# Hybrid attention/DeltaNet block on one core: block read-back moved to SyncE, gate differences and spread moved, other slots for convolutions and FFN input

## What is computed

```
proj = xn @ w_in                       # 2048 x 7184
dn_qkv = silu(causal_dwconv(dn_qkv, dn_conv_w))          # width 4
g = cumsum over a chunk of 64;  decay = exp(g_i - g_j) where i >= j
L = tril(k_beta @ k^T * decay);  T = inv(eye + L)
u = T @ v_beta;  w = T @ (k_beta * exp(g))               # then a scan over chunks
mix = concat(rmsnorm(attention), rmsnorm(o_dn) * silu(z)) @ w_out
ffn: (gelu(gate) * val) @ w_down, with gate, val = split(causal_dwconv(h @ w_up) + b)
```

## Time and profile before

| | |
|---|---|
| median of 3 runs | 1251.06 us (1250.89 to 1254.26) |
| profiled execution, its time | 1252.81 us |
| its span | 1251.1 us |
| TensorE busy | 1226.1 us, 98% |
| VectorE, ScalarE, GpSimd busy | 877.2, 738.8, 214.9 us |
| granted TensorE clock, mean | 0.997 |
| DMA over the span | 183 GB/s |

### The profile page before, as it was taken

The page is one execution under the profiler, slowest core; times in us unless marked ns, Lnnn a source line. Parts: engine busy times, 40 slices in busy tenths (PEclk is TensorE's granted clock), DMA queues, the critical chain, the costliest instruction groups (busy, mean ns, idle before and its releaser), DMA issues.

```text
span 1251.1 us, 20175 instructions
## 1 busy us (share of the span) xinstructions
PE 1226.1 (98%) x6651; PEld 1051.1 (84%) x6651; DVE 877.2 (70%) x1633; ACT 738.8 (59%) x1454; POOL 214.9 (17%) x254
## 2 busy tenths in 40 slices
PE   8899999999999999999999999999999999999997
PEld 6787897889888888788888888888888888888886
DVE  5878866754444754788878888887887885555554
ACT  7767558544867555666566656656656554444442
POOL 1120511141103000022222322222232220000000
PEclk9999999999999999999999999999999999999999
DMA  9647332842443655255455455555555565555551
GB/s 375 254 154 244 138 127 92 251 140 103 148 154 135 218 188 200 103 202 199 173 199 198 168 201 182 189 189 184 195 183 193 194 236 186 186 200 203 185 185 67
DMA packets 35909, 228.91 MB, mean 183 GB/s; under 512 B 6528, under 2 KB 6928, under 8 KB 9232
## 3 DMA queue, kind: packets, MB, share of 16 engines
q1 hardware_dynamic: 34016, 223.50, 50.2%
q10 hardware_dynamic: 1840, 4.71, 1.2%
HBM read 225.96 MB, written 2.24 MB: 182 GB/s over the span
## 4 chain that ended last, share of the span: by engine, by line
PE 85%; DVE 5%; ACT 3%; DMA 3%; issue 2%; POOL 1%; SPq 1%; DVEq 0%; ACTq 0%; POOLq 0%
PE bank L1334 32%; PE bank L1338 16%; PE bank L1362 10%; PE bank L1360 10%; PE bank L1361 10%; DVE w_lo L896 2%; DMA arena<-in_x_tok 2%; DMA arena<-base_rows 1%; DVE arena L917 1%; PE bank L1479 1%; ACT w_hi L464 1%; PE bank L1472 1%; PE bank L1455 1%; PE bank L1639 1%; PE bank L1637 1%
## 5 line engine op out<-in xcount | busy, mean ns | idle before, releaser
L896 DVE TENSOR_TENSOR w_lo<-raw,w_hi 128x512 fp32r<-128x512 f32 x816 | 574.8, 726 | 263.6 <-ACT w_hi L464 259.3
L464 ACT ACTIVATE w_hi<-raw 128x512 fp32r<-128x512 f32 x816 | 502.2, 630 | 356.3 <-PE bank L1334 176.8
L1334 PE MATMUL bank<-xhl,w_hi 128*128 128x512 f32 x2044 | 659.7, 399 | 5.4 <-DVE arena L901 2.7
L1338 PEld LDWEIGHTS bank<-xhl,w_lo 128*128 128x128 f32 x2044 | 384.8, 188 | 88.0
L1338 PE MATMUL bank<-xhl,w_lo 128*128 128x256 f32 x2044 | 402.4, 278 | 0.0
L1334 PEld LDWEIGHTS bank<-xhl,w_hi 128*128 128x128 f32 x2044 | 317.1, 189 | 7.3 <-DVE w_lo L896 3.3
L1361 PE MATMUL bank<-w_lo,ffn_act 128*128 128x512 f32 x336 | 130.7, 389 | 0.0
L1360 PE MATMUL bank<-w_hi,ffn_act 128*128 128x512 f32 x336 | 130.7, 389 | 0.0
L1362 PE MATMUL bank<-w_hi,ffn_act 128*128 128x512 f32 x336 | 130.7, 389 | 0.0
L434 POOL TENSOR_TENSOR arena<-arena,token_scale 128x256 f32<-128x256 f32 x88 | 78.1, 902 | 302.9 <-DVE arena L901 192.5
L1258 DVE SCALAR_TENSOR_TENSOR arena<-arena,fcw 128x256 f32<-128x256 f32 x176 | 85.3, 485 | 23.9 <-DVE arena L1255 1.5
(11 more groups left out here) (239 smaller groups left out, 1005.6 us busy)
## 6 DMA issues: line engine op xcount, KB each, us to landing
raw<-in_wts SPq DMA_DIRECT2D x203, 1024.0 KB, 4.8
xfeat<-in_x SPq DMA_DIRECT2D x4, 512.0 KB, 8.6
arena<-in_x_tok SPq DMA_DIRECT2D x1, 2048.0 KB, 19.8
xfeat<-in_x_tok SPq DMA_DIRECT2D x1, 2048.0 KB, 9.2
arena<-base_rows ACTq DMA_DIRECT2D x4, 512.0 KB
out_y<-xfeat SPq DMA_DIRECT2D x8, 256.0 KB, 2.0
arena<-gate_rows SPq DMA_DIRECT2D x1, 1024.0 KB, 4.2
arena<-in_post_gains ACTq DMA_DIRECT2D x1, 1024.0 KB, 6.1
```

What stands on the lines that cost most here:

```text
L464: nc.scalar.activation(w_hi[:, i % RING, :], raw[:, slot, quarter * PIECE:(quarter + 1) * PIECE], ACT.Copy).then_inc(hi_ready, 1)
L896: V.tensor_tensor(w_lo[:, i % RING, :], raw[:, slot, quarter * PIECE:(quarter + 1) * PIECE], w_hi[:, i % RING, :].bitcast(f32), ALU.subtra ...
L1334: return M(ps[j][:, :], w_hi[:, r % RING, kk * P:(kk + 1) * P], xhl[:, k, :, :].rearrange("p a t -> p (a t)"), start=(k == 0), stop=(k == ...
L1338: return M(ps[j][:, 0:T], w_lo[:, r % RING, kk * P:(kk + 1) * P], xhl[:, CHUNK_K * q + kk, 0, :], start=False, stop=False, skip_group_chec ...
```

## The change

SyncE reads the base blocks back itself, behind its stores and ahead of the next weight chunk. The gate differences of batch 1 are made at places 92 to 95 (before: 100 to 103), and their exponential stands between `qs` and `z1`. VectorE spreads the base columns, at places `_l + 32` and `_l + 33`. Row sums, gates and the turned logits stand one place later. Taps of the convolutions of groups 3 to 5 stand at 1, 4, 7, 10 of their group, the SiLU at 12. In the output norm, one residual tile stands ahead of the last evacuation, both in the mixer and in the FFN. `WARM` is 7.

```diff
-WARM = 8
+WARM = 7
-SILU_AT = [10, 9, 10, 15, 15, 15]
-CONV_AT = [(3, 5, 7, 9)] + [(1, 3, 5, 7)] * 2 + [(1, 5, 9, 13)] * 3
+SILU_AT = [10, 9, 10, 12, 12, 12]
+CONV_AT = [(3, 5, 7, 9)] + [(1, 3, 5, 7)] * 2 + [(1, 4, 7, 10)] * 3
-PLACE = {"ba": 10, "stat": 14, "ba_turn": 16, "scale": 15, "gate": 21, "gcum": 24, "grow": 28}
+PLACE = {"ba": 10, "stat": 15, "ba_turn": 17, "scale": 16, "gate": 21, "gcum": 25, "grow": 28}
...
-        PLACE["spread", _b, _g] = _l + 35
-        PLACE["turn", _b, _g] = _l + 37 + _g
+        PLACE["spread", _b, _g] = _l + 32 + _g
+        PLACE["turn", _b, _g] = _l + 36 + _g
...
+for _i in range(BH):
+    PLACE["dm", _i] = 34 + _i
+    PLACE["dm", BH + _i] = 92 + _i
+PLACE["dexp", 0], PLACE["dexp", 1] = 39, 98
@@ sync, behind the eight stores of a batch
+                sp.wait_ge(s("scratch_in"), 16 * NBLK * (b + 1))
+                for jh in range(2):
+                    rows_ = slice(jh * BASE // 2, (jh + 1) * BASE // 2)
+                    sp.dma_start(block_l[:, rows_].rearrange("p j u i -> p (j u i)"),
+                                 scratch[b].rearrange("(n j) (o x) -> n o j x", j=BASE, o=1)[:, :, rows_, :].rearrange(
+                                     "n o j x -> n o (j x)").to_broadcast([NBLK, BASE, BASE * UNITS * BASE // 2])
+                                 ).then_inc(s(f"block_in{jh}"), 16)
@@ scalar
-                follow(PLACE["load", b])
-                act_e.wait_ge(s("scratch_in"), 16 * NBLK * (b + 1))
...
                 scaled_columns(lambda i: otok[b][:, 2 * i + 1, :], ps[7], EG, 1, "qs_sb")
+                if b == 0:
+                    decay(1)
                 follow(PLACE["z1", b])
@@ vector, behind the last row step (the same product stood on gpsimd)
+                dve.wait_ge(s("base_row"), BASE * (b + 1))
+                for g in range(2):
+                    follow(PLACE["spread", b, g])
+                    V.tensor_tensor(
...
+                if b == 0:
+                    gate_difference(1)
                 follow(PLACE["ks", b])
@@ vector, mixer to FFN
-                out_tile(NB - 1, j)
...
             dve.wait_ge(s("row_root"), 3)
-            dve.wait_ge(s("m_evac"), NJ * NB)
             hidden(1, 0)
+            out_tile(NB - 1, 1)
             hidden(1, 1)
@@ vector, end
-                down_tile(NB - 1, j)
                 dve.wait_ge(s("row_root"), j + 5)
-                dve.wait_ge(s("f_evac"), NJ * (NB - 1) + j + 1)
+                dve.wait_ge(s("f_evac"), NJ * (NB - 1) + j)
                 for c in range(NB):
+                    if c == 1:
+                        down_tile(NB - 1, j)
+                    if c == NB - 1:
+                        dve.wait_ge(s("f_evac"), NJ * (NB - 1) + j + 1)
                     residual(down, 2, j, c * 512, (c + 1) * 512, "y_ready")
```

More of the change, by code:

```diff
@@ L395, in _ @@
                                    pattern=[[0, UNITS], [1, P]], channel_multiplier=-1).then_inc(s("dmask"), 1)
[L396 to L403, removed]
                 for i in range(2 * LEVELS * b, 2 * LEVELS * (b + 1)):
@@ L589, in _, with decay @@
             nc.scalar.activation(col[:, KE, :], col[:, KE, :], ACT.Exp).then_inc(s("gate_col"), 1)
+            def decay(b):
+                follow(PLACE["dexp", b] - 1)
+                act_e.wait_ge(s("ddiff"), BH * b + BH)
+                lot = dm[:, BH * b:BH * b + BH, :]
+                nc.scalar.activation(lot, lot, ACT.Exp).then_inc(s("dexp"), 1)
             for b in range(BATCHES):
                 h0 = BH * b
-                follow(PLACE["dexp", b] - 1)
-                act_e.wait_ge(s("ddiff"), h0 + BH)
-                nc.scalar.activation(dm[:, h0:h0 + BH, :], dm[:, h0:h0 + BH, :], ACT.Exp).then_inc(s("dexp"), 1)
+                if b == 0:
+                    decay(0)
                 for g in range(2):
@@ L1009, in _, with gate_difference @@
             V.tensor_copy(grow, ps[6][0:ALL_UNITS, 2 * P:3 * P]).then_inc(s("grow_sb"), 1)
-            for b in range(BATCHES):
-                h0 = BH * b
-                for h in range(h0, h0 + BH):
+            def gate_difference(b):
+                for h in range(BH * b, BH * b + BH):
                     follow(PLACE["dm", h])
@@ L1019, in _ @@
                     ins.then_inc(s("ddiff"), 1)
+            for b in range(BATCHES):
+                h0 = BH * b
+                if b == 0:
+                    gate_difference(0)
                 follow(PLACE["kt", b, 1] + 2)
@@ L1059, in _ @@
                                     mybir.AxisListType.X, ALU.add).then_inc(s("base_row"), 1)
+                dve.wait_ge(s("base_row"), BASE * (b + 1))
+                for g in range(2):
+                    follow(PLACE["spread", b, g])
+                    V.tensor_tensor(
+                        tmatT[:, 4 * g:4 * g + 4, :].rearrange("p u (b i) -> p u b i", i=BASE),
+                        base_cols[:, 4 * g:4 * g + 4, :].rearrange("p u (o i) -> p u o i", o=1).to_broadcast([P, 4, NBLK, BASE]),
+                        pos_block.rearrange("p (o b i) -> p o b i", o=1, i=BASE).to_broadcast([P, 4, NBLK, BASE]),
+                        ALU.mult).then_inc(s("spread"), 1)
                 i0 = 2 * LEVELS * b
@@ L1193, in _ @@
                         mixer_stat(0)
+                        out_tile(NB - 1, 0)
                     split(IN_GROUPS + c, AHEAD + r)
@@ L1216, in _ @@
             split(UG, 4)
+            dve.wait_ge(s("m_evac"), NJ * NB)
             hidden(1, 3)
```

## The result

| | before | after |
|---|---|---|
| median, both measured together, 6 runs each | 1252.16 us | 1261.78 us |
| ratio | | 1.0069 (95%: 1.0054 to 1.0084) |
| span of the profiled execution | 1251.1 us | 1260.9 us |
| granted TensorE clock, mean | 0.997 | 0.993 |

A forecast was written before the change was run, and what follows sets the result against it. TensorE was taken to bound the kernel, busy 1226.1 of 1251.1 us. Terms summed to 6.05, with 0.15 us for each of four or five waits 6.7 us: 1244.4 from the median, range 1240.5 to 1248.3.

The forecast's parts named there:

- The read-back of batch 0: Moved to SyncE: the 2.8 us wait for `qa` goes, a new 1.1 us wait comes; net +1.7 us.
- my 7.3 us from split to SiLU: ScalarE's estimated work in batch 0 from the split at place 54 to the end of the SiLU.
- the new wait: TensorE waits for the SiLU before batch 0's turned values, near 105 us; forecast 1.1 us.
- the row steps: VectorE's 15 row steps in batch 0 were to begin some 6 us sooner, the blocks being there.
- Rival (c): Slower: SyncE's wait starves the splits, chunk lands at about 111; 13 us lost against 7.8 gained elsewhere, 1256; 5%.
- Second x: Wait for GpSimd's masked operand at 139.6 us, 1.5 us, falls to 0.4; +1.1 us.
- batch 1: Gate differences and exponential moved earlier: bank wait at 210 us stays, the second at 213 goes; +1.0 us.
- The gates: Row sums and gate sums one piece later: +1.4 +1.1 -0.7 = +1.8 us.
- The row sums' 1.4: TensorE does a piece while waiting for the row sums' diagonal: 1.4 of the 2.0 us gained.
- the new 0.7: New wait of TensorE for the cumulative gates near 55 us, charged 0.7 us.
- FFN input: Residual ahead of the last output tile at the FFN's input, no longer behind it; +0.4 us.
- end: Same swap at the kernel's end: the last result leaves about 0.15 us later; -0.15 us.

The follow-up runs named there:

- e5: Changed kernel with 18 dummy multiplications on TensorE ahead of its wait for the SiLU at batch 0's values' turn; 1259.07 us, ratio 1.0063.
- e9: e7 with the SiLU of groups 3 to 5 back at place 15 of its group; 1252.78 us, ratio 1.0007.
- e12: e9 with the taps of groups 3 to 5 back at 1, 5, 9, 13; 1248.16 us, ratio 0.9974.
- e11: Kernel before with only gates, gate differences with their exponential, WARM and both orders of residual and last tile changed; 1247.82 us, ratio 0.9975.
- e7: e1 with ScalarE's read-back issued three places later; 1252.56 us, ratio 1.0008.
- e1: Changed kernel with the read-back back on ScalarE, with its own wait for the stores; 1252.53 us, ratio 1.0001.
- e8: Kernel before with only row sums, gates and turned logits one place later; 1251.43 us, ratio 0.9991.
- e10: e7 with the spread back on GpSimd and the turn one place later; 1255.6 us, ratio 1.0032.
- e15: e14 with GpSimd's masked operands one place earlier in its order; 1245.89 us, ratio 0.9957.
- e13: Kernel before with only the taps of groups 3 to 5 moved from 1, 5, 9, 13 to 1, 4, 7, 10; 1257.05 us, ratio 1.0034.
- e14: e11 with blocks stored twice, two chunks between the store lots, and the read-back on SyncE behind them, on sixteen engines; 1246.36 us, ratio 0.9961.

## Why the prediction was wrong

**The read-back of batch 0 (+1.7 forecast) is the step that failed, in the line "33 packets took 16.6% of 16 engines' 2 us: 161 ns each ... So I take it that eight DMA engines carry it: 256 / 8 x 0.161 = 5.2 us".** Eight engines was right. The 161 ns were not: I read them at the tail of the transfer, where 0.166 x 16 = 2.7 engines were busy on average. With eight under way a packet takes 0.26 us at first and 0.34 on average (8 x 10.9 / 256). The row beside it could have told me: 0.243 x 16 x 17.5 / 272 = 0.25 us a packet over the whole transfer. The read-back took 10.9 us, and the chunk landed at 107.3 and not at 99.1. Of these 8.2 us the packets make 5.7. Another 1.5 are that the read-back was issued at 91.67 and not at 90.2, since the stores began at 84.97, as before, and not at 83.7; about 1 is the first packet and the chunk's own share. All behind it followed as I had written: split, taps, SiLU, values. The terms of my 7.3 us from split to SiLU add up to 7.5, and 7.5 is what it measured (107.33 to 114.87); the new wait was 8.0 us start to start and not 1.1. I also had no term for the same read-back in batch 1, which cost 1.4 us at 247.5. And the row steps did not begin 6 us sooner: the first ran at 110.96, where it had run at 108.56, since the splits ahead of it on VectorE waited for the chunk.

**Rival (c) had this mechanism, at 5%, with a wrong point of decision.** I put even at 106 us, since 7.8 us were to be gained elsewhere. The chunk came at 107.3, the read-back's place cost 9.3 us, and the gain elsewhere was 0. Against it I had "alone, a packet takes 161 ns", the same misread row, and that the 15.8 us had held two chunks. These now stand behind the read-back, and its packets took longest, 0.41 us, while they moved on the other eight engines.

**The half clock** behind the wait, some 2.3 us, was in no term. The windows of the changed kernel and e5 show it.

**Second x (+1.1) and batch 1 (+1.0).** I wrote that the tap at 77 "now stands at 74" and took that for a gain, and suspected the SiLU. e9 clears the SiLU; e12 shows the tap at 74, ahead of the sum and no longer behind it, as the loss. With the old tap places the wait for the operand in batch 0 does go with the spread on VectorE (e12), 1.5 us of idle time, but the turn's waits, 0.4 us in e11 and 1.5 and 0.3 in e12, take 1.4 of it back. Of these 1.4, 1.0 comes with the later read-back of e12, which e7 has against e1 as well. That read-back also takes away `qa`'s 1.3 us. By all its waits e12 has 0.9 us less idle time than e11, and yet the two kernels are equal; what takes it back is not shown. In batch 1 the second bank wait went, as forecast, and the first fell with it: 3.5 to 1.5 us start to start in e11, where I had said that the first stays. In the changed kernel the taps made it 2.6.

**The gates (+1.8)** gave 0.7 to 1.1. The row sums' 1.4 and the new 0.7 were right; the gate column kept 0.9 of its 1.1 us.

**FFN input (+0.4) and end (-0.15).** The wait at the input went from 0.92 to 0.72 us start to start, so 0.2. From TensorE's last multiplication to the end of the span it was 1251.1 - 1243.55 = 7.55 us and is 1260.9 - 1253.21 = 7.69: as forecast.

The sum of the parts without the read-back was to be 5.0 and measures 0.0 in e1 and 3.7 in e11, where taps, SiLU and spread are left out.

## What to carry to other kernels

Take the time of a packet where the queue is as full as it will be in the changed kernel, not at the tail of a transfer; then look at what stands behind it on that queue, and how many engines its slowest dimension gives it. A step moved "earlier" has moved ahead of something: list what was behind it and is now not. Several short waits can be cheaper than one long one of the same sum: TensorE's clock fell behind a wait of 8 us, and in some executions behind one of 2.

## What the runs showed of the hardware

Two transfers of 512 KB whose slowest dimension was 8 took 10.9 us, and 4.4 us with 16 and the source stored twice, at 0.26 us a packet of 4 KB in both at first. On eight engines with weights on the other eight it was 0.41, and 0.16 with 2.7 engines busy on average.

Behind 8 us of TensorE's idle time the granted clock was 0.50 for 5 us; with dummies in the wait it stayed at 1.00. Behind a bank wait of 2.2 us it was 0.72 and then 0.94 in two windows of 5 us (e7), and 1.00 behind the same wait in e1. The profiles of e8 and of e10 to e15 have no window of 5 us below 1.00 before 1240 us, with waits of 3.8 us (e10) and 3.4 (e13) among them.

Kernels whose longest wait between 60 and 300 us was over 3 us (e10, e13) came out at mean clocks of 0.990 to 0.998 from run to run and spread over 4 to 9 us, those under 2 us (e12, e14, e15) at 0.997 to 0.999 and over 2 to 4 us. That the long waits are what lowers the clock in these runs is argued from this, and not shown.
